# Half of the output projection's products worked inside the delta-rule tiles of a two-layer mixer kernel

## The reference

```python
y = concat([gdn, fnet, conv])       # 512 + 256 + 256 columns
x = x + gate1 * (y @ w_out)         # w_out: 1024 x 1024
```

## Time and profile before

| what | value |
|---|---|
| time, median of 3 runs | 4371.61 us |
| lowest and highest run | 4365.52 and 4374.01 us |
| span of the profiled execution | 4365.4 us |
| its instructions | 55131 |
| TensorE matmul busy (PE) | 3693.1 us, 85% |
| TensorE weight loads busy (PEld) | 1903.6 us, 44% |
| VectorE (DVE) | 3006.0 us, 69% |
| ScalarE (ACT) | 1720.2 us, 39% |
| GpSimd (POOL) | 1645.7 us, 38% |

### The profile page before, as it was taken

One profiled execution on the slowest core, in us unless ns is written; L12 is line 12 of the kernel. 1 busy time (PEld: TensorE's weight loads), 2 busy tenths in 40 slices (PEclk: granted clock), 3 DMA queues, 4 the chain that ended last, 5 costly groups with the idle time before them and its releaser, 6 DMA issues. The chain is left out here.

```text
span 4365.4 us, 55131 instructions
## 1 busy us (share of the span) xinstructions
PE 3693.1 (85%) x18945; PEld 1903.6 (44%) x18945; DVE 3006.0 (69%) x6251; ACT 1720.2 (39%) x5270; POOL 1645.7 (38%) x1508
## 2 busy tenths in 40 slices
PE   7998998988888887888886888888898888888777
PEld 3566854533433433433432335775443343343222
DVE  3964666975775875875875885557797687687444
ACT  2223623444344344344342454353444433433333
POOL 0004513443443443444443432352444444444332
PEclk9999999999999999999998999899999999999999
DMA  8360159999999999999999997015999999999997
GB/s 336 122 239 29 37 198 367 416 421 421 418 415 422 414 417 421 407 420 422 410 412 369 408 394 303 2 37 190 404 422 421 421 421 421 421 413 421 422 421 325
DMA packets 238985, 1506.07 MB, mean 345 GB/s; under 512 B 28433, under 2 KB 33617, under 8 KB 71153
## 3 DMA queue, kind: packets, MB, share of 16 engines
q0 software_dynamic: 184320, 1342.26, 74.7%
q1 hardware_dynamic: 54384, 160.28, 9.9%
HBM read 1490.32 MB, written 12.12 MB: 344 GB/s over the span
## 5 line engine op out<-in xcount | busy, mean ns | idle before, releaser
L2831 PE MATMUL ps<-low,pediag 128*128 128x512 f32 x2180 | 1058.7, 615 | 226.1 <-ACT pediag L2741 219.3
L2606 DVE CUSTOM_DVE_ANT_0 low<-low,hc 128x1024 f32<-128x1024 f32 x545 | 667.8, 1225 | 359.3 <-DMA low<-in_experts_dram,eid 342.0
L2585 POOL DMA_INDIRECT low<-in_experts_dram,eid x539 | 595.0, 1104 | 812.4 <-PE ps L2831 783.2
L2733 ACT ACTIVATE low<-peact 128x1 f32<-128x1 f32 x1152 | 232.1, 201 | 1335.0 <-DVE peact L2606 1334.0
L2831 PEld LDWEIGHTS ps<-low,pediag 128*128 128x128 f32 x2180 | 388.9, 192 | 824.5 <-ACT pediag L2741 499.4
L2741 ACT ACTIVATE pediag<-cst,low 128x128 f32<-128x128 f32 x1152 | 462.5, 402 | 42.1 <-PE ps L2831 4.5
L2831 PE MATMUL ps<-wide_a,pediag 128*128 128x512 f32 x640 | 307.8, 612 | 54.4 <-ACT pediag L2741 54.2
L2736 ACT ACTIVATE low<-low,gw 128x1 f32<-128x1 f32 x1152 | 339.1, 294 | 37.4
L2831 PE MATMUL ps<-wide_b,pediag 128*128 128x512 f32 x640 | 303.3, 605 | 50.7 <-ACT pediag L2741 48.5
L2060 PEld LDWEIGHTS ps<-qkvT,arena 128*128 128x128 f32 x2560 | 312.0, 193 | 75.4 <-issue 75.4
L2060 PE MATMUL ps<-qkvT,arena 128*128 128x128 f32 x2560 | 313.1, 276 | 2.4 <-ACT qkvT L2024 2.4
(11 more groups left out here) (497 smaller groups left out, 5773.9 us busy)
## 6 DMA issues: line engine op xcount, KB each, us to landing
pjdot<-in_mod_t_dram SPq DMA_DIRECT2D x64, 512.0 KB, 5.2
arena<-in_w_mod_dram SPq DMA_DIRECT2D x24, 1024.0 KB, 14.4
arena<-in_peer_wq_dram SPq DMA_DIRECT2D x8, 2048.0 KB, 17.1
low<-in_experts_dram,eid POOLq DMA_INDIRECT x609, 8.7
pjw<-in_w_cols_dram SPq DMA_DIRECT2D x18, 512.0 KB, 3.7
plw<-in_w_cols_dram SPq DMA_DIRECT2D x18, 512.0 KB, 8.1
x_rows<-low SPq DMA_DIRECT2D x10, 512.0 KB, 7.7
qkvT<-mod_rows SPq DMA_DIRECT2D x9, 512.0 KB, 7.6
```

Source lines behind the costliest of these rows:

```text
L2585: nc.gpsimd.indirect_dma_start(ring.row(g), None, table, bass.IndirectOffsetOnAxis(eid[:, j % 2, k:k + 1], 0)).then_inc(ring.landed(g), 16)
L2606: nc.vector.tensor_tensor_reduce(out=dot_out if final else ring.row(g)[:, 0:D], in0=ring.row(g)[:, 0:D], in1=hc[:, j % 2, :], scale=1.0, s ...
L2733: nc.scalar.activation(ge[:, g % 2, 0:1], act_v[:, j % 2, k:k + 1], ACT.Gelu_apprx_tanh).then_inc(gelu_ready, 1)
L2831: last = nc.tensor.matmul(ps[:, half, :], diag[:, g % DIAGS, :], ring.row(g)[:, D + half * 512:D + (half + 1) * 512], start=k == 0, stop=k ...
```

## The change

A new class `BranchRows` takes the branch half of every output product out of mix_out. Its products go into gdn_tiles, into PSUM bank 2: `EARLY_LEVELS` says how many k-blocks go between the first products and the updates of each level, and how many after the next tile's inverse is turned (the sixth number). A half has four k-blocks and is worked in one bank, so the first k-block of a half waits for the multiply of the half before it. VectorE multiplies a finished half by the gate and adds it to the token row, ahead of the subtractions of the next level, and SP stores the row and loads the next one. mix_out then loads these rows and adds the delta rule's half in the same way. The gram products move from bank 2 to bank 3, and the turning of the first inverse, which writes bank 3 too, waits for the reach product. Several buffers move, the weights of w_out are now split by rows instead of columns, and the ring's order and the waits of its first gathers are new.

```diff
+EARLY_LEVELS = ((1, 1, 2, 2, 1, 1), (1, 1, 1, 1, 1, 1))
+class BranchRows:
+    BANK = 2
...
+    def issued(self, t, n):
+        return min(t * sum(self.share) + sum(self.share[:n + 1]), self.halves * KD // 2)
...
+    def sp(self, sp):
+        n = len(self.tiles)
+        sp.dma_start(self.w, self.kit.w_out[self.L, H * P:D, :].rearrange("(k p) n -> p k n", p=P)).then_inc(self.w_in, 16)
+        self.load_gate(sp, 0)
+        self.load(sp, 0)
+        for i in range(n):
+            sp.wait_ge(self.added, 2 * (i + 1))
+            sp.dma_start(self.rows(i), self.xb).then_inc(self.saved, 16)
+            if i + 1 in self.turns:
+                self.load_gate(sp, i + 1)
+            sp.wait_ge(self.saved, 16 * (i + 1))
+            if i + 1 < n:
+                self.load(sp, i + 1)
+    def pe(self, pe, t, n):
+        for m in range(self.products, self.issued(t, n)):
+            q, k = divmod(m, KD // 2)
+            i, half = divmod(q, 2)
+            if m == 0:
+                pe.wait_ge(self.w_in, 16)
+            if k == 0 and q:
+                pe.wait_ge(self.gated, q)
+            last = self.nc.tensor.matmul(self.kit.ps[:, self.BANK, :], self.mixT[:, H + k, self.tiles[i], :],
+                                         self.w[:, k, half * 512:(half + 1) * 512], start=k == 0, stop=k == KD // 2 - 1)
+            if k == KD // 2 - 1:
+                last.then_inc(self.prod, 1)
+        self.products = self.issued(t, n)
+    def dve(self, dve, t, n):
+        done = self.issued(t, n - 1) if n else self.issued(t - 1, len(self.share) - 1) if t else 0
+        self.add(dve, done // (KD // 2))
+    def rest(self, dve):
+        self.add(dve, self.halves)
+    def add(self, dve, upto):
+        for q in range(self.sums, upto):
+            i, half = divmod(q, 2)
+            cols = slice(half * 512, (half + 1) * 512)
+            dve.wait_ge(self.gate_in, 16 + 16 * sum(i >= n for n in self.turns))
+            dve.wait_ge(self.prod, q + 1)
+            if q:
+                dve.wait_ge(self.added, q)
+            self.nc.vector.tensor_tensor(self.yb, self.kit.ps[:, self.BANK, :], self.gate[:, cols], ALU.mult
+                                         ).then_inc(self.gated, 1)
+            dve.wait_ge(self.gated, q + 1)
+            dve.wait_ge(self.x_in, 16 * (i + 1))
+            self.nc.vector.tensor_tensor(self.xb[:, cols], self.xb[:, cols], self.yb, ALU.add
+                                         ).then_inc(self.added, 1)
+        self.sums = max(self.sums, upto)
...
                 def turn_inverse(t):
+                    pe.wait_ge(gram_used, t + 1)
...
                             last.then_inc(w_ready, 1)
+                        early.pe(pe, t, n)
                         for d in range(2):
                             pe.wait_ge(w_copied, 2 * NL * t + 2 * n + d + 1)
...
                     if t + 1 < NT:
                         turn_inverse(t + 1)
+                    early.pe(pe, t, NL)
...
                     for n in range(NL):
+                        early.dve(dve, t, n)
                         for d in range(2):
                             dve.wait_ge(upd_ready, 2 * NL * t + 2 * n + d + 1)
...
+                early.rest(dve)
...
-            if row < 4:
+            if row < 2:
                 return HALVES
-            if row > 7:
-                return 1
-            here = [i for i in range(n_tiles) if tiles[i] // 2 == row - 4]
-            return 2 * (max(here) + 1) if here else 1
+            here = [i for i in range(n_tiles) if i // 4 == row - 4]
+            return 2 * (max(here) + 1) if here else 0
...
-                sp.dma_start(w[1], w_out_half(kit, L, 1)).then_inc(w_in, 16)
...
+                def product(q):
+                    i, half = divmod(q, 2)
+                    cols = slice(half * 512, (half + 1) * 512)
+                    pe.wait_ge(copied, n_tiles if q >= 4 else i + 1)
+                    if gated_for(q):
+                        pe.wait_ge(gated, gated_for(q))
+                    for k in range(H):
+                        last = nc.tensor.matmul(ps[:, bank_of(q), :], oT[:, i, k, :], w[:, k, cols],
+                                                start=k == 0, stop=k == H - 1)
+                    last.then_inc(prod_ready, 1)
...
-                branch_part(0)
                 turn(0)
-                scan_part(0)
                 turn(1)
+                product(0)
+                product(1)
                 turn(2)
-                product(1)
                 turn(3)
                 product(2)
...
-                ring = RowRing(first_row, rows, [5, 6, 2, 3, 4, 0, 1, 7], sems[0:RING + 1])
+                ring = RowRing(first_row, rows, [2, 3, 6, 4, 5, 0, 1, 7], sems[0:RING + 1])
...
-                ring = RowRing(first_row, rows + [kit.cst[:, P:P + 2 * D]], [4, 8, 5, 0, 1, 2, 3, 6, 7], sems[0:RING + 2])
+                ring = RowRing(first_row, rows + [kit.cst[:, P:P + 2 * D]], [2, 3, 8, 5, 4, 0, 1, 6, 7], sems[0:RING + 2])
```

More of the change, by code:

```diff
@@ L1430, in gdn_tiles @@
+def gdn_tiles(nc, kit, L, first, hT, qkvT, gate, kt, us, wT, qkd, decs, dts, early):
     G = 2 * H
@@ L1471, in gdn_tiles, with _ @@
         with nc.Block() as block:
+            @block.sync
+            def _(sp):
+                early.sp(sp)
             @block.tensor
@@ L1500, in sums @@
                             col = (4 * d + kind) * NT * H
-                            last = nc.tensor.matmul(ps[:, 3, col:col + NT * H], kit.c(m), gate[:, :, d * H:(d + 1) * H],
+                            last = nc.tensor.matmul(ps[:, 7, col:col + NT * H], kit.c(m), gate[:, :, d * H:(d + 1) * H],
                                                     start=True, stop=True)
@@ L1785, in _, with gdn_scan @@
                     right_keys(t, 1)
-def gdn_scan(nc, kit, L, first, hT, qkvT, kt, us, wT, qkd, decs, dts, o, w0):
+def gdn_scan(nc, kit, L, first, qkvT, kt, us, wT, qkd, decs, dts, o, w0, room):
     NCH = T // CHUNK
@@ L1804, in gdn_scan @@
         sb = lambda n, s: mem.enter_context(nc.sbuf_tensor(f"sc{n}_{L}", s, FP32))
[L1805 to L1809, removed]
+        S, Sd, vn, tail = (room[:, i * D:(i + 1) * D].rearrange("p (d h n) -> p d h n", d=2, h=H) for i in range(4))
+        part = kit.hc[:, 0, 0:GW].rearrange("p (h n) -> p h n", h=H)
         root = sb("root", [P, 1])
@@ L1894, in _ @@
                         dve.wait_ge(part_ready, s - S0 + 1)
-                        nc.vector.tensor_tensor(us[:, s], part[:], bank(2), ALU.add).then_inc(o_ready, 1)
+                        nc.vector.tensor_tensor(us[:, s], part, bank(2), ALU.add).then_inc(o_ready, 1)
                         for c in ready_at.get(s, []) if s == NCH - 1 else ():
@@ L2161, in expert_number, with mix_out @@
         nc.vector.tensor_copy(self.kit.eid[:, j % 2, n], num[:, 0, n]).then_inc(self.eid_ready, 1)
[L2164 removed]
+def mix_out(nc, kit, L, tiles, o, oT, qkvT, zs, z0, w, ring):
     HALVES = 2 * len(tiles)
@@ L2447, in _ @@
                 for g in range(ring.size):
-                    if g:
+                    if g and products_reading(ring.order[ring.place(g)]):
                         pool.wait_ge(prod_ready, products_reading(ring.order[ring.place(g)]))
```

137 lines of the change are left out of this document (70 added, 67 removed).

## The result

The changed kernel takes 4438.07 us (median of 5 runs, 4433.61 to 4443.45) against 4371.61 before: 1.016 times as long, 95% interval 1.0148 to 1.0172, so 66.5 us slower. The forecast was +62.8. The profiled executions (spans of 4365.4 and 4436.2 us) differ by 70.8, by stage as follows; a tile stage runs from the first product of beta to the scan's clearing of its state S, an output stage from VectorE's first instruction in it to the first expert dot.

The account below looks back on a forecast made before the run. TensorE was taken to bound the tiles and fill the late mixer's output. Tiles +50.1 and +30.7, mixer's output -13.3 and -4.7 (layers 0 and 1) sum to +62.8 on the median 4371.6: 4434 us, range 4400 to 4456.

Parts of the forecast that it names:

- The bound: Delta-rule tiles: TensorE runs matmuls in 20.70 of 23.27 us; each moved product costs 0.86 us there.
- Rivals 1 and 2: Tiles: TensorE has room, by weight loads (4379 us) or because slots are really idle and hide products (4364); chance 0.06 each.
- Rival 1: Tiles: weight loads tell TensorE's room, 4.88 us free a tile, so far more cover; +8, 4379 us; chance 0.06.
- Rival 3: Mixer's output pays back all it loses on TensorE, -41.3 and -27.5; +12, 4384 us; chance 0.04.
- Rival 4: Tiles: the row's round trip or the adds hold the subtractions, about 30 us more, 4465 us; chance 0.04.
- Stalls: Tiles: a half's first product waits for VectorE's multiply; layer 0 0.7 and 0.65 us, layer 1 0.7 to 2.7.
- The slots: Tiles: products at 0.86 us plus stalls less covered gaps, 6.65 us for a middle tile of layer 0.
- The tail: End of layer 0's tiles: last multiply, add, row store and its landing 8.4 us, second phase exit 0.6.
- The adds at nothing: Tiles: VectorE's adds after the multiplies cost nothing, as updates come later still; without that cover 0.69 each, 8 us.
- The output stage: Mixer's output gets shorter by 13.3 us in layer 0 and 4.7 in layer 1.
- The expert numbers thus come 4.8 us sooner: Mixer's output, layer 0: second multiply 2.4 us sooner, and 2.4 of VectorE's idle time before the third pick freed.
- Ring and loads at nothing: Expert-row gathers freed from waiting for products (bounds 0 and -3), and the tiles' loads and row round trips: all cost nothing.

Follow-up runs that it names:

- the doubling: Changed kernel with every moved product issued twice (160 in place of 80), nothing else touched; one run, span 4504.4 us.
- the quarter: Changed kernel with only the first of each moved half's four products issued (20 of 80), all else kept; one run, span 4399.5 us.
- the reordered run: Changed kernel with tiles 2 and 3 turned between the first tile's two scan halves in the mixer's output; 4437.23 us, ratio 1.0164.
- the run with the late adds: Changed kernel with products dealt 0, 2, 2, 0, 2, 2 and each half's multiply and add behind the subtractions; 4420.87 us, ratio 1.0107.

## Why the prediction was right, and where not

**The bound.** Right. TensorE fills the tiles, and a moved product costs its own time there: 0.86 us forecast from the output stage's rows, 0.86 measured by doubling.

**Rivals 1 and 2** (room on the array) fall with the doubling, 41.3 us for 48 products, and the quarter. Rival 1 was read from the weight loads' 18.39 us of 23.27; they left 4.88 us a tile that no product could use. The Trainium skill (Perfetto Trace Analysis, Identifying the Most-Contended Engine) judges TensorE's headroom by MFU (the share of its peak arithmetic, not worked out here) and by weight-load time; the forecast named the second alone. On weight-load time this case disagrees: with the products in, the weight loads fill 20.96 us of 30.94, and yet eight more products make that tile 6.87 longer. **Rival 3** (the output stage gives back all of its TensorE time) falls with the kernel that leaves the branch halves out: 17.6 of 69 us. **Rival 4** (adds hold the subtractions) did not happen, but its mechanism is real: as soon as a level had no product beside the add, TensorE idled for 1.54 us ahead of the next one in place of 0.31, and a tile took 30.56 us in place of 29.32.

**Stalls.** Level 0: 0.7 forecast, 0.68 measured. Level 3: 0.65 and 0.43. Layer 1: 2.7 and 2.63 at level 2, 1.0 and 0.50 at level 4. Tile 0's turning of the inverse waited 6.59 us in place of 5.57, the 1.0 that was forecast.

**The slots: mis-sized.** The forecast priced products and left out 0.19 us for entering each slot: six slots a tile give 1.14, so 6.65 + 1.14 - 0.22 (level 3's stall) = 7.57 against 7.67. Over 36 slots in layer 0 that is 6.8 us, over 32 in layer 1 6.1. The remaining 0.10 of the middle tile is the cover at level 2 (0.75 in place of 0.85). Layer 0's first tile grew by 9.1 us, 1.1 more than these terms give, and the last by 9.1, 0.3 more; these remainders were not traced.

**The tail: mis-sized the other way.** From the last copies to the scan I took 8.4 + 0.6; it is 5.4 (551.60 to 557.02) in place of 0.9, so 4.5. The 6.9 us of the earlier trace rows are those of stores in the output stage, where other transfers run (DMA share 0.44 in the earlier trace rows; 0.11 in the changed tile and 0.33 in the tail); this stage's six stores land in 3.9 us by the median of the changed kernel's DMA issues, those of its output stage in 7.1. That the other transfers make the difference was not tested. In the sum this miss offset most of the slots' error in layer 0, which is luck. In layer 1 the 0.6 for a second phase exit did not show: from the last copies to the scan it is 1.31 us, 1.33 before.

**The adds at nothing.** Right in the sum, wrong in the row: 0.69 was priced, 1.30 to 1.55 ran, and 0.54 us of the subtractions' wait was left at level 0.

**The output stage.** -13.3 and -4.7 forecast, -11.2 and -6.7 measured; near in size, in both layers by another way. "The expert numbers thus come 4.8 us sooner" failed in layer 0: the first gather came 0.3 sooner. Both terms of the 4.8 came, 1.9 of 2.4 us at the second multiply and 2.5 of 2.4 from the first pick of experts (MAX8 on VectorE) to the gather, 24.91 us before and 22.41 after; but between that multiply and the first pick 4.1 were lost. The step saw TensorE's and VectorE's orders and not ScalarE's, in which the square stands behind copies that the new order of turns delays (1.8 us, by the reordered run), nor the lower clock behind the idle time (0.9 us more on the turning of h and 1.5 on the first queries). After the first gather, 10.9 us against my 8.5: there the adds stopped waiting for TensorE and wait for rows, as the forecast had it. In layer 1 the first gather came 3.5 us sooner and not 4.7, and 3.2 more came behind it, where the forecast had VectorE busy to the end and priced nothing; the wait for the first dot fell from 9.01 to 5.64 there.

**Ring and loads at nothing.** The row's round trip holds nothing in the tile that was read, and the -2.9 us of layer 0's rest lie within what that row does over the runs (2088.6 to 2096.4).

## What to carry to other kernels

Before work is moved off a full engine, ask what stands next behind it there (here adds and row loads, so that 18 of 69 us came back), and before it is put beside other work, count the receiving engine's time from start to start, not its weight loads. Work fitted into slots has a price per slot as well as per instruction, and a helper instruction ahead of a chain is free only as long as the slot's own work delays that chain. A gap opened ahead of TensorE's next work can cost more than its idle time: here a lower clock followed it, 2.4 us on the next 40 matmuls in layer 0.

## What the runs showed of the hardware

- A VectorE add whose operands all lie in SBUF takes 0.69 us alone and 1.30 to 1.56 where it overlaps GpSimd's tensor operations (446.86 to 448.42 against 446.61 and 447.84 above). GpSimd is slowed too: L1851 takes 1.49 there, and 1.04 in the run with the late adds. In that run a GpSimd operation starts 0.28 us after the add (444.62 against 444.34), the add keeps 0.69, and the GpSimd operation takes 1.54 in place of 1.28; so in these rows it is the later of the two that is slowed. The multiply out of PSUM kept 0.68 to 0.69 in every row read.
- After 4.82 us of idle TensorE the granted clock was 0.50 during the turning of h and 0.70 over the first queries; after 1.39 idle the queries had 0.68; after none and after 0.52 they had 1.00 and took 3.81. The 1.21 us between the turning of h and the queries is the same in all of these. In layer 1 of the changed kernel, after 2.93 idle, the same 32 queries took 6.18.
- Between 64x64 matmuls, one or two products of 128x128 by 512 columns took 0.19 us beyond their own 0.86 us each, once per slot (1.05 with one, 1.91 with two). Whether that is the change of shape was not tested.
